# A pair of experts shares its 128 rows from both ends, in sixteen rounds instead of seventeen

## The chip, the cores and the metric

The kernel runs on one core of a Trainium2 chip. The metric is the device time of one execution in microseconds (us). The core has a matrix engine (TensorE, in the rows PE, with its weight loads as PEld), a vector engine (VectorE, DVE), a scalar engine (ScalarE, ACT), a general engine (GpSimd, POOL) and SyncE (SP), which here only issues DMAs. They run on their own and wait for one another by semaphores.

## What is computed

Two transformer layers on 512 tokens of 1024 features, all in float32. The change lies in the mixture of experts of the first layer; all else keeps its work. Cut to that:

```python
def hierarchical_moe(xn, w_rg, b_rg, w_re, b_re, w_gate, w_up, w_down):
    # 512 tokens; 4 groups of 8 experts; a token takes its best group and there the best 2 experts
    experts = (g_sel[:, None] * EXPERTS_PER_GROUP + top_i).astype(jnp.int32)      # 2 of 32 for each token
    ...
    def expert_block(args):
        xblk, e = args                                                            # rows of x, an expert
        hid = jax.nn.silu(xblk @ w_gate[e]) * (xblk @ w_up[e])                    # 1024 -> 512, twice
        return hid @ w_down[e]                                                    # 512 -> 1024
    ...
    y = jax.ops.segment_sum(yb * row_w[:, None].astype(yb.dtype), row_tok, num_segments=t + 1)[:t]
```

So 1024 pairs of token and expert fall on 32 experts, 32 on average. Worked out from the reference with these inputs, the fullest expert (number 5) has 74 tokens and all others have 64 or fewer; of the pairs (e, e + 16) the fullest has 93 tokens.

## The kernel before

**Weights.** All weights come from one array in units of 128 x 2048 floats (1 MB), in the order of use. An expert has six units (`PER_EXPERT`): two of the gate product, two of the up product, two of the down product.

**A round.** `expert_round` takes two neighbouring experts (`PAIR_UNITS` = 12 units, 12 MB, in `moe_w0` to `moe_w11`). Expert 2e has rows 0 to 63 of a block of 128 rows and expert 2e + 1 rows 64 to 127 (`CAP` = 64). PE turns the block of gathered rows (`turn_rows`, 8 transposes, line 741). In `up_units` each of 32 products (line 756) takes 64 columns of the turned rows `xe` as the held operand and streams 512 columns of a weight unit past it; the products of the two experts alternate and write to the two halves of the partitions of a bank. The gate sum stands in bank 2, the up sum in bank 3. ACT makes `gate` (silu, line 1357) as soon as the gate half is done, DVE multiplies it with bank 3 into `hid` (line 2036), PE turns `hid` (`turn_hidden`, 4 transposes, line 763), ACT and DVE each copy half of it into `hid_t` (lines 1362 and 2041), and `down_units` makes 16 products (line 779) into banks 5 and 6. ACT and DVE copy these to `y_rows`, and POOL scatters the rows to `pair_rows` (line 2477), each to the place of its pair of token and choice. A float32 product stands in the trace as two records of MATMUL, so a round has 64 and 32 of them.

**Where things are started.** SP reloads `moe_w` slot s for the next round when `unit_used` says that its unit of this round was used (line 494). POOL gathers the rows of round e + 2 (line 2467) when those of round e are turned. While the first sums of a round are made, the next round's rows are in `xe`: `turn_rows` of the next round stands between `up_units` and `turn_hidden`.

**The seventeenth round.** 16 rounds take all experts with up to 64 tokens each. What is over is cut into parts of up to 64 rows; a last round (`EXTRA`), which always runs, takes the first two parts, with its weights read again at addresses that SP loads from `over_int` (line 504). Without parts it would run on rows of no token. For more parts there is a branch, `overflowing`, with a loop of 14 turns over `over_weights`.

**Before the first round.** The router's numbers are made on DVE in a chain of small operations, each waiting for the one before (`chain`). The last of them is `dest`, the row of each pair in `slot_table`. POOL then writes the table with 8 indirect DMAs (line 2456), reads it back into `slots` with two DMAs (lines 2460 and 2461), issues the load of `over_slots` (line 2463), and gathers the first rows.

**After the last round** POOL waits for the scatters, SP loads `y_pairs`, and PE adds them to the residual (line 853). Then the second layer begins, whose weights are split into a rounded part and its rest (`w_hi`, `w_lo`) and multiplied three times (lines 556 to 558).

Of the kernel before, what the change touches and what calls it, by code (L numbers as in the profile page):

```python
# [49 lines left out]
U_HG = U_EXTRA + 2 * PER_EXPERT  # L50
# [9 lines left out]
EXTRA = NPAIR  # L60
ROUNDS = NPAIR + 1
PAIR_UNITS = 2 * PER_EXPERT
N_OVER = 14
# [8 lines left out]
def columns(*sizes):  # L72
    at, out = 0, {}
    for name, n in sizes:
# [5 lines left out]
                      ("sel", H1 * P), ("eps", 1), ("iota32", NE), ("lane", NE))  # L80
# [34 lines left out]
def build(nc, x_in, weights_in, constants_in, phase1_in, phase2_in, phase3_in, out):  # L115
    with ExitStack() as ctx:
# [75 lines left out]
        gate = place("gate", [FE], at_b + 16 * KB2)  # L192
        hid = place("hid", [FE], at_b + 17 * KB2)
        hid_t = place("hid_t", [4, P], at_b + 18 * KB2)
# [10 lines left out]
        def overflowing(eng):  # L205

            eng.wait_ge(dest_ready, 1)
            return eng.value_load(over_int[0:1, 2 + N_OVER:3 + N_OVER]) > 0

# [18 lines left out]
        over_cmp, over_e = tiny("over_cmp", [2 + N_OVER, NE]), tiny("over_e", [2 + N_OVER])  # L228
        over_int = tiny("over_int", [N_OVER + 3], I32)
# [11 lines left out]
        slot_table = nc.dram_tensor("slot_table", [MAIN + (2 + N_OVER) * CAP, 2], I32, kind="Internal").ap()  # L241
# [5 lines left out]
        TABLE = (MAIN + (2 + N_OVER) * CAP) * 2  # L247
# [182 lines left out]
        STORED_FROM, LANDED_FROM = 16 * (NPAIR // 2 + 1), 16 * (NPAIR // 2)  # L430
# [37 lines left out]
        def _(sp):  # L468
# [29 lines left out]
            sp.wait_ge(dest_ready, 1)  # L498
            over_unit = [sp.value_load(over_int[0:1, b:b + 1]) * PER_EXPERT + U_MOE for b in range(2)]
            for j in range(PER_EXPERT):  # L500
                for b in range(2):
                    s = 2 * j + b
                    sp.wait_ge(unit_used, U_EXTRA - PAIR_UNITS + s + 1)
                    sp.dma_start(moe_w[s][:], weights_in[bass.ds(over_unit[b] + j, 1)].rearrange("u p n -> p (u n)")) \
                        .then_inc(raw_landed[s], 16)

            for j in range(RAW):
                sp.wait_ge(unit_used, U_EXTRA + j + 1)
                sp.dma_start(raw[:, j], weights_in[U_EXTRA + j]).then_inc(raw_landed[j], 16)
# [38 lines left out]
        def _(pe):  # L548
# [196 lines left out]
            def up_units(e):  # L745

                for j in range(4):
# [39 lines left out]
            def expert_round(e, next_rows):  # L787
# [8 lines left out]
                pe.wait_ge(hid_ready, e + 1)  # L796
                turn_hidden()
# [4 lines left out]
            with pe.Fori(0, NPAIR // 2) as i:  # L802
                for b in range(2):
                    expert_round(i * 2 + b, (1 - b, i * 16 + 16 * (b + 1)))
            expert_round(EXTRA, None)


            with pe.If(overflowing(pe)):
                with pe.Fori(0, N_OVER) as v:
# [14 lines left out]
                    for c in range(4):  # L824
                        mm = nc.tensor.transpose(bank[4][:, c * P:c * P + P], hid[:, c * P:c * P + P], ident)
# [3 lines left out]
                    for c in range(4):  # L829
                        for half in range(2):  # L830
                            w = (c % 2) * D + half * 512
                            mm = nc.tensor.matmul(bank[5 + half][:], hid_t[:, c], over_weights[:, c // 2, w:w + 512],
# [1925 lines left out]
```

## Time and profile before

| | |
|---|---|
| time, median of 3 runs | 2318.77 us (2316.73 to 2321.3) |
| the profiled execution | 2321.49 us, of which the span is 2319.8 us |
| PE busy | 2080.0 us (90%), 10252 records of MATMUL |
| DVE, ACT, POOL busy | 39%, 29%, 16% |
| weights of the experts | 204 transfers of 1 MB, queued 25.2 us each (median) |
| first product of the experts, end of the last | 357.5 us, 874.2 us |

The profile cuts the span into 40 slices of 58 us. The experts fill slices 7 to 15; there the DMA engines are busy throughout and move 421 to 422 GB/s, while PE shows 7 to 8 tenths. Of the chain of work that ended last, 17% is the transfer of `moe_w`; nearly all else of it is PE.

### The profile page before, as it was taken

The page shows a single profiled execution, that of the slowest core. Times are in us where ns is not written, and L with a number is a line of the kernel's source. Part 1 is how long each engine was busy: PE and PEld are TensorE (multiplying, and loading weights), DVE is VectorE, ACT ScalarE, POOL GpSimd, SP SyncE. Part 2 cuts the span into 40 slices and gives each one's busy share as a digit, 9 for nine tenths or more (in the row PEclk, how much of TensorE's full clock was granted, in tenths as well). Part 3 has the DMA queues.
Part 4 walks back from the last instruction along what each step waited for, and adds up shares of the span by engine and source line. Part 5 has one row for each costly group of instructions (what it writes and reads, how often), then busy time and mean ns, then how long its engine had stood idle before and what let it go on. Part 6 is the DMA issues. An engine that isn't in the chain of part 4 may idle for free.

```text
span 2319.8 us, 25950 instructions
## 1 busy us (share of the span) xinstructions
PE 2080.0 (90%) x10252; PEld 1544.2 (67%) x10252; DVE 904.7 (39%) x1162; ACT 664.5 (29%) x840; POOL 363.3 (16%) x354
## 2 busy tenths in 40 slices
PE   6996828877777778999989999999999999999999
PEld 5894713322223227888867888887789987888887
DVE  5535250000000005677765432334775434333332
ACT  3433120000000004666644221223222323221222
POOL 0000020000000001554531110111343101100100
PEclk9997968999999999999989999999999999999999
DMA  5220247999999993121112222223222322222220
GB/s 203 78 105 0 86 181 305 421 422 421 421 421 421 421 410 154 55 73 55 55 62 91 91 95 104 91 90 109 91 74 98 140 73 91 91 91 98 96 97 37
DMA packets 57640, 378.10 MB, mean 163 GB/s; under 512 B 8944, under 2 KB 9040, under 8 KB 13904
## 3 DMA queue, kind: packets, MB, share of 16 engines
q1 hardware_dynamic: 51120, 363.02, 40.0%
q0 software_dynamic: 6432, 13.83, 1.7%
q8 instruction: 64, 1.05, 0.2%
q14 instruction: 24, 0.20, 0.0%
HBM read 370.99 MB, written 15.26 MB: 167 GB/s over the span
## 4 chain that ended last, share of the span: by engine, by line
PE 65%; DMA 18%; DVE 7%; issue 5%; ACT 3%; POOL 1%; SPq 0%; DVEq 0%; POOLq 0%; ACTq 0%
PE bank L556 18%; PE bank L557 18%; PE bank L558 18%; DMA moe_w<-weights_in 17%; PE bank L779 3%; PE bank L756 2%; DVE o_tmp L2185 1%; PE bank L853 1%; DVE k_dec L2161 1%; PE bank L675 1%; PE bank L1176 1%; POOL k_rot L2574 1%; PE bank L954 1%; PE bank L966 1%; DVE ws L2170 0%
## 5 line engine op out<-in xcount | busy, mean ns | idle before, releaser
L556 PE MATMUL bank<-u_hi,w_hi 128*128 128x512 f32 x1152 | 463.3, 402 | 0.7 <-issue 0.7
L557 PE MATMUL bank<-u_lo,w_hi 128*128 128x512 f32 x1152 | 455.5, 395 | 0.0
L558 PE MATMUL bank<-u_hi,w_lo 128*128 128x512 f32 x1152 | 455.1, 395 | 0.0
L1702 DVE TENSOR_TENSOR w_lo<-raw,w_hi 128x2048 fp32r<-128x2048 f32 x96 | 233.1, 2428 | 299.9 <-ACT w_hi L1227 299.7
L756 PE MATMUL bank<-moe_w,xe 128*64 128x512 f32 x1088 | 262.2, 629 | 88.9 <-DMA moe_w<-weights_in 87.7
L756 PEld LDWEIGHTS bank<-moe_w,xe 128*64 128x64 f32 x1088 | 91.1, 144 | 259.1 <-issue 259.0
L1227 ACT ACTIVATE w_hi<-raw 128x2048 fp32r<-128x2048 f32 x96 | 183.7, 1913 | 273.2 <-PE bank L558 272.3
L556 PEld LDWEIGHTS bank<-u_hi,w_hi 128*128 128x128 f32 x1152 | 216.5, 188 | 54.2 <-issue 3.5
L557 PEld LDWEIGHTS bank<-u_lo,w_hi 128*128 128x128 f32 x1152 | 216.5, 188 | 52.6 <-issue 2.4
L558 PEld LDWEIGHTS bank<-u_hi,w_lo 128*128 128x128 f32 x1152 | 216.2, 188 | 53.0
L556 PE MATMUL bank<-w_hi,u_hi 128*128 128x256 f32 (+1 forms) x640 | 191.5, 299 | 7.3 <-issue 7.3
L557 PE MATMUL bank<-w_lo,u_hi 128*128 128x256 f32 (+1 forms) x640 | 188.8, 295 | 0.0
L558 PE MATMUL bank<-w_hi,u_lo 128*128 128x256 f32 (+1 forms) x640 | 188.6, 295 | 0.0
L2563 POOL TENSOR_TENSOR f_gate<-f_gate,rms 128x512 f32<-128x512 f32 x44 | 57.0, 1296 | 566.5 <-ACT f_gate L1574 566.5
L2036 DVE TENSOR_TENSOR hid<-gate,bank 128x512 f32<-128x512 f32 x17 | 11.7, 689 | 339.0 <-PE bank L756 339.0
L779 PE MATMUL bank<-moe_w,hid_t 128*64 128x512 f32 x544 | 123.6, 596 | 17.8 <-ACT hid_t L1362 6.4
L556 PEld LDWEIGHTS bank<-w_hi,u_hi 128*128 128x128 f32 x640 | 122.0, 191 | 11.5 <-issue 8.3
L557 PEld LDWEIGHTS bank<-w_lo,u_hi 128*128 128x128 f32 x640 | 122.0, 191 | 3.2
L558 PEld LDWEIGHTS bank<-w_hi,u_lo 128*128 128x128 f32 x640 | 121.9, 190 | 3.1
L2280 DVE TENSOR_TENSOR f_hid<-f_gate,bank 128x512 f32<-128x512 f32 x44 | 30.3, 689 | 212.6 <-PE bank L558 212.6
L556 PE MATMUL bank<-hid_hi,w_hi 128*128 128x512 f32 x272 | 107.5, 395 | 0.1
L557 PE MATMUL bank<-hid_lo,w_hi 128*128 128x512 f32 x272 | 107.4, 395 | 0.0
(415 smaller groups left out, 2756.3 us busy)
## 6 DMA issues: line engine op xcount, KB each, us to landing
moe_w<-weights_in SPq DMA_DIRECT2D x204, 1024.0 KB, 25.2
raw<-weights_in SPq DMA_DIRECT2D x128, 1024.0 KB, 4.8
y_pairs<-pair_rows SPq DMA_DIRECT2D x4, 1024.0 KB, 7.7
res<-x_in SPq DMA_DIRECT2D x1, 2048.0 KB, 7.8
token_rows<-xn POOLq DMA_DIRECT2D x1, 2048.0 KB, 7.0
v_rows<-vals SPq DMA_DIRECT2D x2, 1024.0 KB, 5.7
vals<-v_rows SPq DMA_DIRECT2D x2, 1024.0 KB, 6.8
out<-out_tile SPq DMA_DIRECT2D x4, 512.0 KB, 2.6
```

Source lines behind the costliest of these rows:

```text
L556: nc.tensor.matmul(out_ap, a_hi, b_hi, start=first, stop=False)
L557: nc.tensor.matmul(out_ap, a_hi, b_lo, start=False, stop=False)
L558: return nc.tensor.matmul(out_ap, a_lo, b_hi, start=False, stop=last)
L675: mm = nc.tensor.matmul(bank[4 + b // 2][:, at:at + VH], dec_at(j, b * P, b * P + P), vm[:, j, h * VH:h * VH + VH], start=b % 2 == 0 and j ...
L756: mm = nc.tensor.matmul(bank[2 + j // 2][rows, :], xe[:, c, rows], moe_w[2 * j + b][:, w], start=c == 0, stop=c == KC - 1)
L779: mm = nc.tensor.matmul(bank[5 + half][rows, :], hid_t[:, c, rows], moe_w[2 * j + b][:, w], start=c == 0, stop=c == 3)
L853: mm = nc.tensor.matmul(of_block(c, b), y_pairs[b][:, k, c * P:c * P + P], share_diag[:, k, b], start=False, stop=b == TB - 1 and k == 1)
L954: mm = nc.tensor.matmul(bank[4 + n % 2][:, t], left, right, start=True, stop=True)
L1227: nc.scalar.activation(w_hi[:, n % 2], raw[:, n % RAW], ACT.Copy).then_inc(hi_ready, 1)
L1702: nc.vector.tensor_tensor(w_lo[:, n % 2], raw[:, n % RAW], w_hi[:, n % 2].bitcast(F32), ALU.subtract) \
L2280: nc.vector.tensor_tensor(f_hid[s][:], f_gate[s][:], bank[2 * s + 1][:], ALU.mult).then_inc(f_prod, 1)
L2563: nc.gpsimd.tensor_tensor(f_gate[n][:], f_gate[n][:], rms[:], ALU.mult).then_inc(f_gated, 1)
```

## The change

Experts e and e + 16 share a round. Expert e fills the 128 rows from the front, expert e + 16 from the back (constants `seat` and `stride`), each up to the `room` that is left, at least 64 rows. Both experts' products are made for all 128 rows: two gate banks (2, 3) and two up banks (4, 7). `mine` (1 or 0 for a row and an expert, from the number of rows of expert e) is multiplied in when `hid` is made, so that a row of the one expert gives zero in the `hid` of the other, and the down products of both add up in the same banks 5 and 6. The round `EXTRA` and its 12 transfers go, the branch for what is over (now 16 turns) stays, and the units of the two experts of a round are laid next to each other by the host.

```diff
-U_HG = U_EXTRA + 2 * PER_EXPERT
+U_HG = U_EXTRA
-ROUNDS = NPAIR + 1
+ROUNDS = NPAIR
...
-            sp.wait_ge(dest_ready, 1)
-            over_unit = [sp.value_load(over_int[0:1, b:b + 1]) * PER_EXPERT + U_MOE for b in range(2)]
-            for j in range(PER_EXPERT):
-                for b in range(2):
-                    s = 2 * j + b
-                    sp.wait_ge(unit_used, U_EXTRA - PAIR_UNITS + s + 1)
-                    sp.dma_start(moe_w[s][:], weights_in[bass.ds(over_unit[b] + j, 1)].rearrange("u p n -> p (u n)")) \
-                        .then_inc(raw_landed[s], 16)
...
                         for b in range(2):
-                            rows = slice(CAP * b, CAP * b + CAP)
-                            mm = nc.tensor.matmul(bank[2 + j // 2][rows, :], xe[:, c, rows], moe_w[2 * j + b][:, w],
+                            mm = nc.tensor.matmul(bank[(2 + b, 4 + 3 * b)[j // 2]][:], xe[:, c], moe_w[2 * j + b][:, w],
                                                   start=c == 0, stop=c == KC - 1)
...
-            def turn_hidden():
-                for c in range(4):
-                    mm = nc.tensor.transpose(bank[4 if c < 2 else 7][:, c % 2 * P:c % 2 * P + P], hid[:, c * P:c * P + P],
-                                             ident)
-                mm.then_inc(hid_turned, 1)
+            def turn_hidden(e):
+
+                for b in range(2):
+                    pe.wait_ge(hid_ready, e * 2 + b + 1)
+                    for c in range(4):
+                        mm = nc.tensor.transpose(bank[2 + b][:, c * P:c * P + P], hid[b][:, c * P:c * P + P], ident)
+                    mm.then_inc(hid_turned, 1)
...
                             for b in range(2):
-                                rows = slice(CAP * b, CAP * b + CAP)
-                                mm = nc.tensor.matmul(bank[5 + half][rows, :], hid_t[:, c, rows], moe_w[2 * j + b][:, w],
-                                                      start=c == 0, stop=c == 3)
+                                mm = nc.tensor.matmul(bank[5 + half][:], hid_t[b][:, c], moe_w[2 * j + b][:, w],
+                                                      start=c == 0 and b == 0, stop=c == 3 and b == 1)
...
                 act.wait_ge(unit_used, u0 + 4)
-                nc.scalar.activation(gate[:], bank[2][:], ACT.Silu).then_inc(silu_ready, 1)
+                for n in range(2):
+                    nc.scalar.activation(gate[n][:], bank[2 + n][:], ACT.Silu).then_inc(silu_ready, 1)
...
-                act.wait_ge(hid_turned, e + 1)
-                nc.scalar.activation(hid_t[:, 0:2], bank[4][:, 0:2 * P].rearrange("p (c t) -> p c t", c=2), ACT.Copy) \
+                act.wait_ge(hid_turned, e * 2 + 1)
+                nc.scalar.activation(hid_t[0][:], bank[2][:].rearrange("p (c t) -> p c t", c=4), ACT.Copy) \
                     .then_inc(hid_t_left, 1)
...
-                dve.wait_ge(silu_ready, e + 1)
                 dve.wait_ge(unit_used, u0 + 8)
-                nc.vector.tensor_tensor(hid[:], gate[:], bank[3][:], ALU.mult).then_inc(hid_ready, 1)
+                for n in range(2):
+                    dve.wait_ge(silu_ready, 2 * e + n + 1)
+                    nc.vector.scalar_tensor_tensor(hid[n][:], gate[n][:], mine[:, n, e:e + 1], bank[4 + 3 * n][:],
+                                                   ALU.mult, ALU.mult).then_inc(hid_ready, 1)
...
-                dve.wait_ge(hid_turned, e + 1)
-                nc.vector.tensor_copy(hid_t[:, 2:4], bank[7][:, 0:2 * P].rearrange("p (c t) -> p c t", c=2)) \
+                dve.wait_ge(hid_turned, 2 * e + 2)
+                nc.vector.tensor_copy(hid_t[1][:], bank[3][:].rearrange("p (c t) -> p c t", c=4)) \
                     .then_inc(hid_t_right, 1)
...
             pool.dma_start(slots[:, 0:NPAIR], slot_table[0:MAIN].rearrange("(s e) c -> s e c", s=P)).then_inc(slots_landed, 16)
-            pool.dma_start(slots[:, EXTRA], slot_table[MAIN:MAIN + P]).then_inc(slots_landed, 16)
-            pool.wait_ge(slots_landed, 48)
-            pool.dma_start(over_slots[0:CAP], slot_table[MAIN + P:].rearrange("(v s) c -> s v c", s=CAP)).then_inc(slots_landed, 16)
+            pool.wait_ge(slots_landed, 32)
...
             gather(0)
             gather(1)
+            pool.dma_start(over_slots[0:CAP], slot_table[MAIN:].rearrange("(v s) c -> s v c", s=CAP)).then_inc(slots_landed, 16)
```

The rounds on DVE, a loop before, are written out one by one. On PE, at the end of `up_units` in the loop of rounds, this stood in a row (`con` is the identity, `moe_w_103` and so on are the slots of weights, a row of a float32 product is one product, and its first shape is the held columns by the streamed ones):

```order
1310 L756 MATMUL bank<-moe_w_103,xe 64x512
1311 L756 MATMUL bank<-moe_w_104,xe 64x512
1312 L794 ISA
1313 L741 MATMUL bank<-con,x_rows 128x128 [waits x_gathered1]
1314 L741 MATMUL bank<-con,x_rows 128x128 x7
1315 L763 MATMUL bank<-con,hid 128x128 [waits hid_ready]
1316 L763 MATMUL bank<-con,hid 128x128 x3
1317 L779 MATMUL bank<-moe_w_105,hid_t 64x512 [waits raw_landed8,raw_landed9,hid_t_right,hid_t_left]
1318 L779 MATMUL bank<-moe_w_106,hid_t 64x512
```

The same place on PE now:

```order
1310 L746 MATMUL bank<-moe_w_106,xe 128x512
1311 L746 MATMUL bank<-moe_w_107,xe 128x512
1312 L785 ISA
1313 L732 MATMUL bank<-con,x_rows 128x128 [waits x_gathered1]
1314 L732 MATMUL bank<-con,x_rows 128x128 x7
1315 L754 ISA
1316 L756 MATMUL bank<-con,hid_95 128x128 [waits hid_ready]
1317 L756 MATMUL bank<-con,hid_95 128x128 x3
1318 L754 REGISTER_ALU
1319 L756 MATMUL bank<-con,hid_96 128x128 [waits hid_ready]
1320 L756 MATMUL bank<-con,hid_96 128x128 x3
1321 L770 MATMUL bank<-moe_w_108,hid_t_97 128x512 [waits raw_landed8,raw_landed9,hid_t_right,hid_t_left]
```

The number of products of a round is the same, all are 128 wide instead of 64, and a second set of four transposes with a wait of its own stands ahead of the down products. On DVE a round was, in the round `EXTRA` at the end (it turns no rows for a next round):

```order
268 L2036 TENSOR_TENSOR hid<-gate,bank 128x512 [waits unit_used,silu_ready]
269 L2041 COPY hid_t<-bank 128x256 [waits hid_turned]
270 L2045 COPY y_rows<-bank 128x512 [waits unit_used,y_free0]
```

The first round on DVE now:

```order
259 L2045 SCALAR_TENSOR_TENSOR hid_95<-gate_93,mine,bank 128x512 [waits silu_ready,unit_used]
260 L2045 SCALAR_TENSOR_TENSOR hid_96<-gate_94,mine,bank 128x512 [waits silu_ready]
261 L2036 COPY xe<-bank 128x512 [waits xe_turned]
262 L2051 COPY hid_t_98<-bank 128x512 [waits hid_turned]
263 L2055 COPY y_rows<-bank 128x512 [waits unit_used,y_free0]
```

Two products of 512 columns stand where one stood, and the copy into `hid_t` has 512 columns instead of 256. On POOL, from the last indirect writes of the table to the first gathers, before:

```order
14 L2456 DMA slot_table<-pairs,dest 3072x2 x7
15 L2460 DMA slots<-slot_table 128x32 [waits table_written]
16 L2461 DMA slots<-slot_table 128x2
17 L2463 DMA over_slots<-slot_table 64x14x2 [waits slots_landed]
18 L2467 DMA x_rows<-token_rows,slots 128x1024 x2
```

and now:

```order
14 L2464 DMA slot_table<-pairs,dest 3072x2 x7
15 L2468 DMA slots<-slot_table 128x32 [waits table_written]
16 L2473 DMA x_rows<-token_rows,slots 128x1024 [waits slots_landed]
17 L2473 DMA x_rows<-token_rows,slots 128x1024
18 L2480 DMA over_slots<-slot_table 64x16x2
```

One read of the table is gone, and the other that isn't needed at once stands behind the gathers. On DVE the six operations that make the numbers for what is over stood ahead of `dest`; they now stand behind it, with the ones that make `mine`, and six other small ones (for `room`, and `row` in two steps) are new in the chain ahead of it.

## Rows read from the trace of the kernel before

**Rows 1.** The page: busy tenths, clock and DMA in 40 slices.

```profile
PE   6996828877777778999989999999999999999999
...
PEclk9997968999999999999989999999999999999999
DMA  5220247999999993121112222223222322222220
GB/s 203 78 105 0 86 181 305 421 422 421 421 421 421 421 410 154 55 73 55 55 62 91 91 95 104 91 90 109 91 74 98 140 73 91 91 91 98 96 97 37
```

**Rows 2.** Chain of work that ended last, in order of time: start, us, what.

```profile
357.53 16.45 PE bank L756 x64
...
420.88 5.20 PE bank L756 x16
...
494.20 3.67 PE bank L779 x16
498.65 27.14 DMA moe_w<-weights_in
525.92 3.67 PE bank L779 x16
...
840.17 3.67 PE bank L779 x16
844.49 25.94 DMA moe_w<-weights_in
870.57 3.67 PE bank L779 x16
```

**Rows 3.** Timeline: start, us, engine, line, operation, count, idle before; a round without DMA waits.

```profile
383.06 13.93 PE L756 MATMUL bank<-moe_w,xe 128*64 128x512 f32 x64
...
400.00 7.09 PE L779 MATMUL bank<-moe_w,hid_t 128*64 128x512 f32 x32 [0.72 <-ACT hid_t L1362]
...
406.89 7.07 PE L756 MATMUL bank<-moe_w,xe 128*64 128x512 f32 x32
```

**Rows 4.** Timeline of PE: a float32 product with 128 held and 512 streamed columns.

```profile
920.38 1.88 PE L996 MATMUL bank<-late_diag,con 128*128 128x512 f32 x4
```

**Rows 5.** The instructions of line 756, then of 779: duration in ns min/median/max.

```profile
L756 PE MATMUL bank<-moe_w,xe x1088: 592/592/1116, 357.5 to 863.7; 128*64 128x512 f32 x182
...
L779 PE MATMUL bank<-moe_w,hid_t x544: 592/592/644, 376.2 to 873.6; 128*64 128x512 f32 x182
```

**Rows 6.** Timeline of one handoff from the up to the down products.

```profile
426.01 1.09 PE L741 MATMUL bank<-con,x_rows 128*128 128x128 f32 x8
426.14 0.69 DVE L2036 TENSOR_TENSOR hid<-gate,bank 128x512 f32<-128x512 f32 x1 [18.32 <-PE bank L756]
...
426.94 0.60 PE L763 MATMUL bank<-con,hid 128*128 128x128 f32 x4
427.14 0.60 ACT L1350 ACTIVATE xe<-bank 128x512 f32<-128x512 f32 x1 [12.55 <-PE bank L741]
427.14 0.69 DVE L2028 COPY xe<-bank 128x512 f32<-128x512 f32 x1 [0.31 <-PE bank L741]
427.64 0.38 ACT L1362 ACTIVATE hid_t<-bank 128x256 f32<-128x256 f32 x1
427.75 0.41 DVE L2041 COPY hid_t<-bank 128x256 f32<-128x256 f32 x1
...
428.27 1.94 PE L779 MATMUL bank<-moe_w,hid_t 128*64 128x512 f32 x8 [0.72 <-ACT hid_t L1362]
```

**Rows 7.** Timeline ahead of the first round: DVE, then POOL.

```profile
331.07 0.69 DVE L1993 TENSOR_TENSOR over_cmp<-over_end,con 128x512 f32<-128x512 f32 x1
...
333.31 0.17 DVE L2002 CAST dest<-dest_f 128x8 int32<-128x8 f32 x1
...
346.87 0.56 POOL L2461 DMA_DIRECT2D slots<-slot_table  x1
349.20 0.82 POOL L2463 DMA_DIRECT2D over_slots<-slot_table  x1 [1.77 <-DMA slots<-slot_table]
350.33 1.07 POOL L2467 DMA_INDIRECT x_rows<-token_rows,slots  x1 [0.30 <-issue]
```

**Rows 8.** Scatters of line 2477, issue to landing; the last of them is in the chain at 875.89.

```profile
DMA to landing us min/median/max: 5.1/8.3/9.1
```

More of the change, by code:

```diff
@@ L59 @@
 NPAIR = NE // 2
-EXTRA = NPAIR
-ROUNDS = NPAIR + 1
+ROUNDS = NPAIR
 PAIR_UNITS = 2 * PER_EXPERT
-N_OVER = 14
+N_OVER = 16
 MAGIC = 12582912.0
@@ L191, in build @@
         xe = place("xe", [KC, P], at_b + 12 * KB2)
-        gate = place("gate", [FE], at_b + 16 * KB2)
-        hid = place("hid", [FE], at_b + 17 * KB2)
-        hid_t = place("hid_t", [4, P], at_b + 18 * KB2)
+        gate = [place(f"gate{b}", [FE], at_b + (16 - 2 * b) * KB2) for b in range(2)]
+        hid = [place(f"hid{b}", [FE], at_b + (17 - 2 * b) * KB2) for b in range(2)]
+        hid_t = [place(f"hid_t{b}", [4, P], at_b + (18 + b) * KB2) for b in range(2)]
         y_rows = place("y_rows", [2, D], at_b + 20 * KB2)
@@ L824, in _ @@
                     for c in range(4):
-                        mm = nc.tensor.transpose(bank[4][:, c * P:c * P + P], hid[:, c * P:c * P + P], ident)
+                        mm = nc.tensor.transpose(bank[4][:, c * P:c * P + P], hid[0][:, c * P:c * P + P], ident)
                     mm.then_inc(over_products, 1)
@@ L1366, in expert_round @@
                 nc.scalar.activation(y_rows[:, b, 0:512], bank[5][:], ACT.Copy).then_inc(y_left, 1)
-            with act.Fori(0, NPAIR // 2) as i:
+            with act.Fori(0, NPAIR // 2 - 1) as i:
                 for b in range(2):
                     expert_round(i * 2 + b, i * (2 * PAIR_UNITS) + (U_MOE + PAIR_UNITS * b), b, i * 16 + 16, False)
-            expert_round(EXTRA, U_EXTRA, 0, 16 * (NPAIR // 2 + 1), True)
+            for b in range(2):
+                expert_round(NPAIR - 2 + b, U_EXTRA - PAIR_UNITS * (2 - b), b, 16 * (NPAIR // 2), b == 1)
             split(U_HG)
@@ L1381, in _ @@
                     act.wait_ge(over_products, v * 4 + 2)
-                    nc.scalar.activation(gate[:], bank[2][:], ACT.Silu).then_inc(over_copies, 1)
+                    nc.scalar.activation(gate[0][:], bank[2][:], ACT.Silu).then_inc(over_copies, 1)
                     act.wait_ge(over_products, v * 4 + 3)
-                    nc.scalar.activation(hid_t[:], bank[4][:].rearrange("p (c t) -> p c t", c=4), ACT.Copy) \
+                    nc.scalar.activation(hid_t[0][:], bank[4][:].rearrange("p (c t) -> p c t", c=4), ACT.Copy) \
                         .then_inc(over_copies, 1)
@@ L1974, in _ @@
             before, count = before_all[:], so_far[:, TB - 1]
-            chain(nc.vector.tensor_scalar(n_over[:], count, 1.0, -0.5 - CAP / 2, ALU.max, ALU.add))
+            for n in range(2):
+                last = nc.vector.tensor_scalar(room[:, n * NPAIR:(n + 1) * NPAIR], count[:, (1 - n) * NPAIR:(2 - n) * NPAIR],
+                                               -1.0, float(P), ALU.mult, ALU.add)
+            chain(last)
+            chain(nc.vector.tensor_scalar(room[:], room[:], float(CAP), None, ALU.max))
+            chain(nc.vector.tensor_tensor(n_over[:], count, room[:], ALU.subtract))
+            chain(nc.vector.tensor_scalar(n_over[:], n_over[:], 1.0 - CAP, CAP / 2 - 0.5, ALU.max, ALU.add))
             chain(nc.vector.tensor_scalar(n_over[:], n_over[:], 1.0 / CAP, MAGIC, ALU.mult, ALU.add))
@@ L1980, in _, with per_token @@
             chain(nc.vector.tensor_tensor(over_start[:], over_end[:], n_over[:], ALU.subtract))
-            chain(nc.vector.tensor_scalar(over_start[:], over_start[:], float(CAP), float(MAIN - CAP), ALU.mult, ALU.add))
-            chain(nc.vector.tensor_scalar(over[:], before, float(CAP), None, ALU.is_ge))
-            chain(nc.vector.tensor_tensor(lift[:], before, over_start[:].unsqueeze(1).to_broadcast([P, TB, NE]), ALU.add))
-            lane = cols(con, C_COLS, "lane").unsqueeze(1).to_broadcast([P, TB, NE])
-            chain(nc.vector.scalar_tensor_tensor(row[:], before, float(NPAIR), lane, ALU.mult, ALU.add))
+            chain(nc.vector.tensor_scalar(over_start[:], over_start[:], float(CAP), float(MAIN), ALU.mult, ALU.add))
+            chain(nc.vector.tensor_tensor(over_start[:], over_start[:], room[:], ALU.subtract))
+            def per_token(tile):
+                return tile.unsqueeze(1).to_broadcast([P, TB, NE])
+            nc.vector.tensor_tensor(over[:], before, per_token(room[:]), ALU.is_ge)
+            nc.vector.tensor_tensor(lift[:], before, per_token(over_start[:]), ALU.add)
+            chain(nc.vector.tensor_tensor(row[:], before, per_token(cols(con, C_COLS, "stride")), ALU.mult))
+            chain(nc.vector.tensor_tensor(row[:], row[:], per_token(cols(con, C_COLS, "seat")), ALU.add))
             chain(nc.vector.tensor_tensor(lift[:], lift[:], row[:], ALU.subtract))
@@ L2045, in expert_round @@
                 nc.vector.tensor_copy(y_rows[:, b, 512:1024], bank[6][:]).then_inc(y_right, 1)
-            with dve.Fori(0, NPAIR // 2) as i:
-                for b in range(2):
-                    expert_round(i * 2 + b, i * (2 * PAIR_UNITS) + (U_MOE + PAIR_UNITS * b), b, i * 16 + 16, False)
-            expert_round(EXTRA, U_EXTRA, 0, 16 * (NPAIR // 2 + 1), True)
+            for e in range(NPAIR):
+                expert_round(e, U_MOE + PAIR_UNITS * e, e % 2, 16 * (e // 2 + 1), e == NPAIR - 1)
             split(U_HG)
@@ L2057, in _ @@
                     dve.wait_ge(over_copies, v * 4 + 2)
-                    nc.vector.tensor_tensor(hid[:], gate[:], bank[3][:], ALU.mult).then_inc(over_hid, 1)
+                    nc.vector.tensor_tensor(hid[0][:], gate[0][:], bank[3][:], ALU.mult).then_inc(over_hid, 1)
             for b in range(TB):
```

62 lines of the change are left out of this document (34 added, 28 removed).

## The prediction

> **What bounds the kernel now.** I read the slices of the page first: in slices 7 to 15, the experts, the DMA engines are busy throughout at 421 to 422 GB/s while PE shows 7 to 8 tenths [rows 1]. So I went to the chain of work that ended last, in order of time. From the third round on it is made of one pattern: 26 to 27 us of moe_w transfers, then the 16 records of the last down unit [rows 2]. From 494.20 to 840.17 there are eleven such rounds, 345.97 / 11 = 31.45 us each: the rate at which 12 MB of weights arrive. The PE work of a round is smaller. Where no transfer is awaited, the 64 records of the up products start at 383.06 and last 13.93 us, and the 32 of the down products take 406.89 - 400.00 = 6.89 us from their first start to the first start of the next round [rows 3]. With the handoff between them (below, 2.26 us) that makes some 23 us of PE against 31.45 us of DMA, 8 us of slack in a round. What matters is what the change does to these 23 us.
>
> **Part 1: the products become 128 wide.** This is the large term. In the kernel before, 32 records of 64 held columns take 6.89 us, 0.215 us a record [rows 3]. One record of itself lasts 592 ns [rows 5], and the two experts' records alternate and write different halves of the partitions: they run beside each other. The same product with 128 held columns stands once in the trace: four records of line 996 in 1.88 us, which is three distances and one duration of 0.592 us, so (1.88 - 0.59) / 3 = 0.43 us a record [rows 4]. That is twice the 0.215, which is what two streams side by side against one would give. The change leaves the count of products alone and makes all of them 128 wide, so nothing can run beside them: 96 records x 0.43 = 41.3 us a round, where it was 20.6. That rows 4 has four records only is a weakness of this term; the bounds below take it in.
>
> A rule of the Trainium skill speaks against this. "TensorE: Matmul & The Clock Gate", section "Back-to-back issue gap", gives a sustained rate of about 131 ns for a 512-column matmul in a real stream, less than its formula for one alone; and "FP8 and Floating Point Precision" counts four passes for a true float32 product, two for each of our records. By these, an estimate, a record would cost 262 ns and a round 96 x 0.262 = 25.2 us of products, which would still lie under the transfers. The trace disagrees as far as it goes (0.43 us in rows 4).
>
> **Part 2: the handoff from up to down.** Before, it is 428.27 - 426.01 = 2.26 us from the first transpose of the next rows to the first down product [rows 6]. Now, from that transpose as zero and with the durations of these rows: hid of the first expert on DVE from 0.13 to 0.82, that of the second right behind until about 1.43, xe's copy until about 2.05; PE turns the second hid from 1.54 (DVE's end plus the 0.11 that the rows show between 426.83 and 426.94); its copy can start 0.70 later, as ACT's did (426.94 to 427.64), at 2.24, and takes 0.69 us for 512 columns, as xe's does; PE starts 0.11 after that, at 3.04. ACT's two copies of 0.60 end by then. The second silu lies under the up products, which now take 27 us. So 3.0 us, +0.8. Bounds: 2.3, if DVE's parts overlap more than I think, and 4.5, if a semaphore costs more.
>
> **A round** is then 41.3 + 3.0 = 44.3 us of PE, against 31.45 us of transfers. Transfers are no longer awaited: each slot is refilled from the moment it was used, and its next use comes a round, 44 us, later; the gathers have over 27 us. The 8 us of slack and the 31.45 us of the removed round are gone against 12.9 us more in each of sixteen rounds.
>
> **Part 3: the sum of the stage.** 16 x 44.3 = 708.8 us. The first round starts on a PE that has idled: its 64 records took 16.45 us against 13.93 at the full clock [rows 2, 3], +2.5 us, and I keep that, since the clock comes back by time. 711.3 us, where the kernel before has 870.57 + 3.67 - 357.53 = 516.7 us [rows 2]. That is **+194.6 us**.
>
> **Part 4: ahead of the first round.** dest no longer waits for the six operations between 331.07 and 333.31 (2.24 us); six others of 0.22 us on average (some of 128 elements, 0.3) are in its chain, +1.3. The read of slots that lands last was issued 0.56 us after the first, and over_slots held up the gather from 349.20 to 350.33, 1.13 us [rows 7]. Together -0.9 - 0.6 - 1.1 = **-2.6 us**; nothing else was late there, for PE had all weights of the round. The work that is now behind dest has 20 us until DVE is wanted. Bounds: -1 and -3.5.
>
> **Part 5: behind the last round.** The last scatter takes 5.1 us, the smallest of all, on the seventeenth round, which holds 10 rows of tokens; it will hold 93. The median of 8.3 comes from a time when the DMA engines were full [rows 8]. I take 5.8, **+0.7 us**, bounds 0 and 3.2. The wider table of constants and the written-out loop on DVE I take as nothing: DVE waits most of a round, and if fetching its code were late by a microsecond, that would stand in the handoff's bound.
>
> **Sum:** +194.6 - 2.6 + 0.7 = +192.7 us. The profiled execution took 2321.49 us (span 2319.8), so by its own time 2514.2; the median of the runs shown is 2.7 us lower, 2318.77, and so I forecast **2511.5 us**.
>
> **The rivals.**
>
> *Wide products cost less, and DMA stays the bound.* If a record of 128 held columns cost under (31.45 - 3.0) / 96 = 0.296 us, the round would be hidden under its transfers, and the change would do nothing but take one round away: 2318.8 - 31.45 - 1 (part of the start) + 0.7 (the last scatter) = 2287 us. For it speaks that what a record of 592 ns shares with its neighbour isn't shown by any row, and the rule above. Against it stands rows 4. This is the case on the other side; it decides at 0.296 us a record. 4%.
>
> *The clock falls in every handoff.* The handoff becomes 3 us of transposes and waiting. In the kernel before the clock does fall now and then after a wait: 16 records took 5.20 us instead of 3.67 [rows 2], 1.5 us lost, and the longest record of line 756 is 1116 ns. With such a fall in each of the sixteen rounds it is 16 x 1.5 = +24 us, 2536 us. Against it: in 17 rounds no down product, which come right behind the handoff, was over 644 ns [rows 5], and the up products behind these ran at full speed at 406.89 [rows 3]. The skill's page on TensorE, section "Part 4: PE-mode transpose", says that transposes don't count as busy for the clock gate, which would speak for this rival; the rows of the 17 handoffs do not bear it out. 8%.
>
> *The branch for what is over is taken.* It would run 16 turns with 6 MB each, one behind the other: at 421 GB/s 15 us of transfers, and 48 records x 0.43 = 21 us of products, some 36 us or more a turn, +570 us. The loads of the experts speak against it: the fullest pair has 93 tokens of 128. 1%.
>
> *The forecast:* PE bounds the stage at about 44 us a round. 87%.
>
> **The numbers.** Around the likeliest: the price of a record from 0.427 to 0.435 us gives -5 to +8; the handoff's bounds -11 to +24; start and tail -1.6 to +4. They will not all fall on one side. With the rival of the clock the range is **2499 to 2542 us**. What it leaves out is the case of cheap products (4%), the branch (1%), and the edges of the rest. Chances: faster by over 0.2% 4%, within 0.2% (about what a measurement of this kernel can tell from no change) 1%, slower by more 95%.
>
> **What would show it.** The product rows of the two lines should read 128*128 with a distance of 0.43 us, so busy times of about 440 us for up (1024 records) and 220 us for down (512). The idle time of PE that transfers end should all but vanish from the stage; the bandwidth there should fall from 421 to about 12.6 MB / 44.3 us = 284 GB/s plus the rows, and the transfers should land sooner than 25 us after their issue. PE's share in these slices should be 9 tenths at the full clock. First to last product: about 711 us. It would be wrong if the wide records stood closer than 0.43 us, if the handoff were not near 3 us, or if the clock in the stage were clearly under full.

## The result: 2514.7 us, 8.4% slower

| | median | runs | lowest to highest |
|---|---|---|---|
| before | 2319.39 us | 4 | 2316.73 to 2321.3 |
| after | 2514.66 us | 4 | 2513.03 to 2517.4 |

The ratio is 1.0844, with a 95% interval of 1.0825 to 1.0863. The forecast was 2511.5 us, with a range of 2499 to 2542.

### The profile page after: what moved, and what is told of

Same layout as the page of the kernel before. It is cut to its first block, busy times and chain, and to the rows that moved or that the text cites. A ratio compares the mean times of both kernels' runs of the same rounds, so it can differ in the third digit from the quotient of the medians.

```text
span 2515.6 us, 25808 instructions
## 1 busy us (share of the span) xinstructions
PE 2372.2 (94%) x10208; PEld 1715.7 (68%) x10208; DVE 917.8 (36%) x1184; ACT 673.2 (27%) x851; POOL 364.4 (14%) x351
## 4 chain that ended last, share of the span: by engine, by line
PE 47%; DVE 4%; issue 4%; ACT 2%; POOL 0%; DMA 0%; DVEq 0%; POOLq 0%
PE bank L547 14%; PE bank L549 14%; PE bank L548 14%; DVE o_tmp L2193 1%; DVE k_dec L2169 1%; PE bank L844 1%; PE bank L1167 1%; PE bank L945 1%; PE bank L957 0%; POOL k_rot L2581 0%; DVE ws L2178 0%; PE bank L1115 0%; ACT L1481 0%; PE bank L1112 0%; PE bank L903 0%
## 5 line engine op out<-in xcount | busy, mean ns | idle before, releaser
L746 PE MATMUL bank<-moe_w,xe 128*128 128x512 f32 x1024 | 444.1, 595 | 1.2 <-DVE xe L2036 1.2
L746 PEld LDWEIGHTS bank<-moe_w,xe 128*128 128x128 f32 x1024 | 195.9, 191 | 246.4 <-issue 246.4
L770 PE MATMUL bank<-moe_w,hid_t 128*128 128x512 f32 x512 | 223.6, 595 | 13.3 <-ACT hid_t L1354 13.3
L770 PEld LDWEIGHTS bank<-moe_w,hid_t 128*128 128x128 f32 x512 | 96.3, 190 | 131.2 <-issue 114.5
L2045 DVE SCALAR_TENSOR_TENSOR hid<-gate,mine,bank 128x512 f32<-128x512 f32 x32 | 22.5, 745 | 430.6 <-PE bank L746 430.6
L2484 POOL DMA_INDIRECT pair_rows<-y_rows,slots x16 | 16.1, 1006 | 685.0 <-DVE y_rows L2055 685.0
```

What stands on the lines that cost most here:

```text
L746: mm = nc.tensor.matmul(bank[(2 + b, 4 + 3 * b)[j // 2]][:], xe[:, c], moe_w[2 * j + b][:, w], start=c == 0, stop=c == KC - 1)
L770: mm = nc.tensor.matmul(bank[5 + half][:], hid_t[b][:, c], moe_w[2 * j + b][:, w], start=c == 0 and b == 0, stop=c == 3 and b == 1)
```

## The profile after

The page of the changed kernel, with the rows that answer to [rows 1]: busy tenths of PE, granted clock and DMA in 40 slices, each now 63 us.

```profile
PE   6995749999999999999999999999999999999999
...
PEclk9997879999999999999999999999999999999999
DMA  4220337877777777431112122222312322222221
GB/s 187 95 74 36 144 141 282 310 299 283 305 286 301 295 290 302 169 140 51 67 68 74 51 101 85 99 99 85 118 68 100 116 86 86 99 91 93 101 84 51
```

In slices 7 to 16, which the experts fill, PE shows 9 tenths where it had 7 or 8, the granted clock is at 9 tenths or more, and the DMA engines are at 7 or 8 tenths with 282 to 310 GB/s where they had up to 422. The two have changed places as the bound. In the chain that ended last, moe_w's transfers, 17% before, no longer appear: the page has

```profile
PE 47%; DVE 4%; issue 4%; ACT 2%; POOL 0%; DMA 0%; DVEq 0%; POOLq 0%
...
L746 PE MATMUL bank<-moe_w,xe 128*128 128x512 f32 x1024 | 444.1, 595 | 1.2 <-DVE xe L2036 1.2
...
L770 PE MATMUL bank<-moe_w,hid_t 128*128 128x512 f32 x512 | 223.6, 595 | 13.3 <-ACT hid_t L1354 13.3
...
moe_w<-weights_in SPq DMA_DIRECT2D x192, 1024.0 KB, 6.4
```

(line, engine, operation, shapes and count | busy us, mean ns | idle before it and what ended it; the last line is KB and us from issue to landing). The shares of the chain do not add up to the span, which it only follows back through the second layer; the groups are the better reading here. The products of a record are 128 wide, their busy times are 444.1 and 223.6 us, and of the idle time ahead of them no part was ended by a transfer of weights. A transfer lands 6.4 us after its issue instead of 25.2.

The timeline of the second round answers to [rows 3] and [rows 6]: start, us, engine, line, operation.

```profile
383.91 1.04 PE L732 MATMUL bank<-con,x_rows 128*128 128x128 f32 x8
384.11 1.41 DVE L2045 SCALAR_TENSOR_TENSOR hid<-gate,mine,bank 128x512 f32<-128x512 f32 x2 [30.00 <-PE bank L746]
384.91 1.31 PE L756 MATMUL bank<-con,hid 128*128 128x128 f32 x8
384.98 0.60 ACT L1341 ACTIVATE xe<-bank 128x512 f32<-128x512 f32 x1 [13.52 <-PE bank L732]
385.43 0.68 DVE L2036 COPY xe<-bank 128x512 f32<-128x512 f32 x1
385.61 0.60 ACT L1354 ACTIVATE hid_t<-bank 128x512 f32<-128x512 f32 x1
386.26 0.69 DVE L2051 COPY hid_t<-bank 128x512 f32<-128x512 f32 x1
387.06 13.97 PE L770 MATMUL bank<-moe_w,hid_t 128*128 128x512 f32 x32 [0.83 <-ACT hid_t L1354]
400.87 27.63 PE L746 MATMUL bank<-moe_w,xe 128*128 128x512 f32 x64
...
428.33 1.04 PE L732 MATMUL bank<-con,x_rows 128*128 128x128 f32 x8
```

The 64 up records last 27.63 us, (27.63 - 0.59) / 63 = 0.429 us from one to the next; the handoff is 387.06 - 383.91 = 3.15 us; a round is 428.33 - 383.91 = 44.4 us.

**Where the 195.8 us of span came from**, by the two profiled executions (spans of 2319.8 and 2515.6 us):

| stretch | before | after | difference |
|---|---|---|---|
| start to the first product of the experts | 357.5 | 354.5 | -3.1 |
| first to last product of the experts | 516.7 | 712.9 | +196.2 |
| last product to the first of y_pairs | 12.8 | 11.1 | -1.7 |
| from there to the end (second layer) | 1432.8 | 1437.1 | +4.3 |

The last row stands at work that the change does not touch. It got runs of its own.

## The experiments

Ten kernels ran. The kernel before was timed beside each group of them (medians of 2317.8 to 2320.6 us).

**1. The width alone taken back.** All of the change but the width of the products (this kernel is called narrow below):

```diff
-mm = nc.tensor.matmul(bank[(2 + b, 4 + 3 * b)[j // 2]][:], xe[:, c], moe_w[2 * j + b][:, w],
+rows = slice(CAP * b, CAP * b + CAP)
+mm = nc.tensor.matmul(bank[(2 + b, 4 + 3 * b)[j // 2]][rows, :], xe[:, c, rows], moe_w[2 * j + b][:, w],
...
-mm = nc.tensor.matmul(bank[5 + half][:], hid_t[b][:, c], moe_w[2 * j + b][:, w], start=c == 0 and b == 0, ...)
+mm = nc.tensor.matmul(bank[5 + half][rows, :], hid_t[b][:, c, rows], moe_w[2 * j + b][:, w], start=c == 0, ...)
```

> The changed kernel with its sixteen rounds, its two gate, up and hidden banks and all else, but each product 64 wide again: expert e for rows 0 to 63, expert e + 16 for rows 64 to 127 (the rows of expert 5 beyond 64 are left out of its products). This takes the width alone back. Theory (the width makes the +196 us of the stage, all else is small and a gain): the stage is bound by its transfers again, 16 x 31.45 us with the faster first rounds, about 485 us where it was 712.9, so 2514.7 - 712.9 + 485 = 2287 us; the handoff of 3.1 us, the second hidden bank and the written-out loop are covered. Rival (part of the loss is in the handoff and the doubled work of DVE and ACT): above 2300 us.

Measured: 2294.23 us, ratio 0.9884 (0.9868 to 0.9901). The width is the loss; all else of the change together is a gain of 1.2%. That is under the rival's bound of 2300, but 7 us over the 2287 I gave. The trace has the stage at 354.1 to 841.0, 486.9 us, close to the 485. The rest is behind it. The last scatter came while transfers of the next stage's weights still filled the DMA engines (the last was issued at 820.8 us, with 25.2 us to landing), and POOL waited 5.66 us after its issue where it waited 3.44 in the changed kernel; and the second layer was long again (1439.1 us; see experiment 6). The timeline of narrow, then of the changed kernel:

```profile
842.70 0.99 POOL L2486 DMA_INDIRECT pair_rows<-y_rows,slots  x1 [29.42 <-DVE y_rows L2057]
...
849.34 0.10 POOL L2512 MEMSET y_mark<- 128x8 int32 x1 [5.66 <-issue]
```

```profile
1069.06 0.99 POOL L2484 DMA_INDIRECT pair_rows<-y_rows,slots  x1 [43.42 <-DVE y_rows L2055]
...
1073.49 0.10 POOL L2510 MEMSET y_mark<- 128x8 int32 x1 [3.44 <-issue]
```

**2. Narrow records without a neighbour.** Both experts' products to rows 0 to 63 (`rows = slice(0, CAP)`).

> The changed kernel with 64 wide products, but both experts' products go to rows 0 to 63 (rows 64 to 127 are left out). The records have the same shape as in the kernel before, 128*64 by 128x512, and their number is the same, but none has a neighbour in the other half of the array. Theory (0.215 us a record is two streams side by side at 0.43 each, the price hangs on streamed columns and passes, not on the held width): 0.43 us a record, about 2515 us, as the changed kernel. Rival (a record with 64 held columns is cheaper in itself): 0.215 us a record, 2287 us.

Measured: 2513.56 us (two runs, 2512.80 and 2514.32), the changed kernel's time. Its timeline has records of the same shape as in the kernel before, at the price of the wide ones:

```profile
429.45 13.92 PE L772 MATMUL bank<-moe_w,hid_t 128*64 128x512 f32 x32 [0.83 <-ACT hid_t L1356]
...
443.20 27.63 PE L747 MATMUL bank<-moe_w,xe 128*64 128x512 f32 x64
```

So a record with 64 held columns and no neighbour is no cheaper than one with 128. The 0.215 us a record of the kernel before were two streams of 0.43 us in the two halves of the array, as the theory had it. The rival is out by 226 us.

**3. The halves one after the other.**

```diff
-for k in range(4):
-    for b in range(2):
+for b in range(2):
+    for k in range(4):
```

(the same in the down products, on top of experiment 1).

> As narrow, with the halves of both experts, but a unit's products of expert e all come first and then those of expert e + 16 (8 records of one half, then 8 of the other), instead of by turns. Theory (records only run beside a neighbour in the other half that comes right behind, in order): only the records at a change of half overlap, about 96 x 7/8 x 0.43 = 36 us of products a round, 39 with the handoff, 2514.7 - 712.9 + 16 x 39.3 + 2 = 2433 us. Rival one (matmuls are taken out of order over 8 records): 2287 us. Rival two (no overlap is left at all): 2515 us.

Measured: 2295.96 us (2292.87 and 2299.05). My theory, that only neighbours in the program run beside each other, is wrong by 137 us. Rival one gave the right time, but not quite for its reason. The weight loads of the down products (start, busy, count in a row; each belongs to a record, and the first row holds the loads of the first two):

```profile
489.60 0.19 PEld L772 LDWEIGHTS bank<-moe_w,hid_t 128*64 128x64 f32 x2 [1.04 <-ACT hid_t L1356]
490.08 0.14 PEld L772 LDWEIGHTS bank<-moe_w,hid_t 128*64 128x64 f32 x1 [0.29 <-issue]
490.51 0.14 PEld L772 LDWEIGHTS bank<-moe_w,hid_t 128*64 128x64 f32 x1 [0.29 <-issue]
490.94 0.14 PEld L772 LDWEIGHTS bank<-moe_w,hid_t 128*64 128x64 f32 x1 [0.29 <-issue]
491.37 0.19 PEld L772 LDWEIGHTS bank<-moe_w,hid_t 128*64 128x64 f32 x3 [0.29 <-issue]
491.80 0.19 PEld L772 LDWEIGHTS bank<-moe_w,hid_t 128*64 128x64 f32 x2 [0.23 <-issue]
492.23 0.19 PEld L772 LDWEIGHTS bank<-moe_w,hid_t 128*64 128x64 f32 x2 [0.23 <-issue]
```

The first four distances of 0.43 us bring one record each; then they come in twos, though eight records of one half stand ahead of the first of the other. Records of one half do not run beside each other (experiment 2). So the first record of the second half starts with the fifth of the first half, ahead of three that stand before it in the program, and from there both halves are busy. So little is lost. A round that waits for no transfer takes 424.94 - 398.83 = 26.1 us by its first transposes, against 23.8 by turns (experiment 5):

```profile
398.83 1.09 PE L732 MATMUL bank<-con,x_rows 128*128 128x128 f32 x8
...
424.94 1.09 PE L732 MATMUL bank<-con,x_rows 128*128 128x128 f32 x8
```

Where 16 up records wait for a transfer they take 5.39 us against 3.65, since each such group starts with one half alone. The idle time of PE that transfers end ahead of the up products shrinks from 75.2 us in narrow to 12.4 us here. The transfers are still the bound, and so the time does not move. That PE's queue holds a few records for each half is my reading of this row of counts; the runs show the overlap and its four records, not how it is made.

**4. The width alone added to the kernel before.** `matmul(bank[2 + j // 2][:], xe[:, c], ...)` in its seventeen rounds.

> The kernel before with its seventeen rounds and only the products made 128 wide (both experts' products are made for all rows and add up in the one bank, so the sums are not those of the reference). The width alone, without the rest of the change. Theory: 17 x (41.3 + 2.3) + 2 = 743 us of stage where it was 516.7, so 2319 + 226 = 2545 us. Rival (wide products cost so much only with the changed banks): less than 2500 us.

Measured: 2538.61 us (2537.87 and 2539.36), ratio 1.0946 (1.0926 to 1.0966). The chain of work that ended last, in order of time, has the rounds at 43.47 us where 43.6 was expected:

```profile
403.50 27.47 PE bank L755 x64
446.97 27.47 PE bank L755 x64
490.44 27.47 PE bank L755 x64
```

The stage is 741.8 us (743 expected). Most of the 6 us that are missing are behind the stage: 10.6 us to the first y_pairs product instead of 12.8, and 1428.0 us from there instead of 1432.8. With experiment 1 this gives all four cases:

| | seventeen rounds | sixteen rounds |
|---|---|---|
| 64 wide | 2319 | 2294 |
| 128 wide | 2539 | 2515 |

The width costs 220 us with either number of rounds. The rest of the change brings 24 to 25 us at either width. At 64 wide that is above all one round of transfers (31 us) less; at 128 wide it is one round of PE (43 us) less, against sixteen longer handoffs.

**5. A quarter of the transfers.** From the second round on `moe_w[s][:, 0:512]` alone is loaded.

> The changed kernel, but from the second round on each transfer of weights brings only 512 of the 2048 columns of its unit (the others keep the first round's weights). It asks whether transfers still bound any part of the stage. Theory (PE alone bounds it): nothing moves, 2513 to 2517 us. Rival (PE's reads of weights and the DMA writes get in each other's way, or some unit is still awaited): some us faster, 2505 or less.

Measured: 2515.32 us (2514.92 and 2515.72). A quarter of the bytes leaves the time where it was: transfers bound nothing in the changed kernel, and their writes at some 300 GB/s cost PE nothing that can be seen.

> As narrow (64 wide, expert 5's rows beyond 64 left out), with a quarter of the weights' transfer from the second round on. It shows PE's own time of a narrow round. Theory: 96 x 0.215 + 3.1 = 23.7 us a round, stage 16 x 23.7 + 2 = 381 us, 2514.7 - 712.9 + 381 = 2183 us, and so 7.7 us of slack a round in narrow. Rival (ACT and DVE, or the gathers and scatters, come up as the next bound): above 2200 us.

Measured: 2187.71 us (2186.87 and 2188.56), 5 us over the theory's figure and under the rival's 2200. The rounds are 464.36 - 440.55 = 23.8 us by their first transposes:

```profile
440.55 1.09 PE L733 MATMUL bank<-con,x_rows 128*128 128x128 f32 x8
...
464.36 1.09 PE L733 MATMUL bank<-con,x_rows 128*128 128x128 f32 x8
```

PE's own round is 23.8 us when narrow and 44.4 when wide, and the transfers' round of 31.45 us lies between them. That is the whole case: of the 20.6 us that the change adds to a round of PE, the first 7.6 were free, and the other 13.0 were paid sixteen times.

**6. Four microseconds at 128 bytes.** The second layer took 4.3 us longer in the changed kernel, and 1 to 6 us longer in all kernels of the experiments above that were made from it (the 4 to 6 in the next expectation leaves out the two shortest). Its products of line 548, `hid_lo` by `w_hi`, have a mean of 397 ns where the kernel before has 395. The one thing that had changed for them was the place of arrays: the table of constants grew from 1345 to 1378 columns, and all that is placed behind it moved by 128 bytes in each partition (places are rounded to 32 bytes). So 33 unused columns went into the kernel before:

```diff
-                      ("sel", H1 * P), ("eps", 1), ("iota32", NE), ("lane", NE))
+                      ("sel", H1 * P), ("eps", 1), ("iota32", NE), ("lane", NE), ("pad", 33))
```

> The kernel before with 33 unused columns behind its table of constants, as many as the change adds. Nothing reads them; they move the parameters and the arrays behind them by 128 bytes in each partition. In all kernels made from the changed one the three products of lines 547 to 549 last 397 ns where they last 394 to 395 in the kernel before, and the time from the first y_pairs product to the end is 4 to 6 us longer. Theory (the moved addresses do it): 394 becomes 397 here too, and the time is 4 us longer, 2323 to 2324 us. Rival (chips differ, or something else of the change): no change beyond 1 us for the longer load of constants.

Measured: 2322.66 us in 11 runs (2320.30 to 2323.54) against 2318.77 in 15 (2316.23 to 2321.26), ratio 1.0015 (1.0006 to 1.0024). And the other way round, the changed kernel with its three new tables put where nothing moves:

> The changed kernel with seat, stride and index moved from the table of constants into the second table of parameters, which is shorter than the room it has, and the first table padded to its former size, so that every array stands at the address that it has in the kernel before. Theory (addresses): 394 ns again and 4 us less, about 2511 us. Rival: 2515 us.

Measured: 2507.26 us (2506.51 to 2508.90), 7.4 us less than the changed kernel, more than expected. The two were not timed side by side; against the kernel before beside each, the ratios are 1.0811 (1.0795 to 1.0828) and 1.0844 (1.0825 to 1.0863), so the size of this difference is known less well than that of the 3.9 us above. The groups of this one product, of the kernel before, then with the pad, of the changed kernel, and of it with the tables moved:

```profile
L557 PE MATMUL bank<-hid_lo,w_hi 128*128 128x512 f32 x272 | 107.4, 395 | 0.0
```

```profile
L557 PE MATMUL bank<-hid_lo,w_hi 128*128 128x512 f32 x272 | 107.8, 396 | 0.0
```

```profile
L548 PE MATMUL bank<-hid_lo,w_hi 128*128 128x512 f32 x272 | 107.9, 397 | 0.0
```

```profile
L549 PE MATMUL bank<-hid_lo,w_hi 128*128 128x512 f32 x272 | 107.5, 395 | 0.0
```

The effect is shown; its cause is not. The starts in the traces give its size. In the second layer some 4470 records stream 512 columns of an array of activations (`u`, `hid` and the like) past a held piece of `w_hi` or `w_lo`. They stand 233.3 ns apart in all four kernels with the tables in their first place, and 234.2 ns in all eight where they are moved: 0.9 ns each, 4.0 us in all, which is what the pad costs. The activations lie behind the table and moved; `w_hi` and `w_lo` lie ahead of it and did not. The 231 records of 512 columns that stream a weight past held activations do not get slower (233.3 and 233.1 ns). That points at the place of the streamed array, but no run moved one array alone. Of the 7.4 us of the kernel with the tables put back, these records explain 4.0; the rest is not explained. Single profiled executions scatter by about 3 us around this: the second layer is 1428.0 to 1434.6 us long in the four with the tables in their first place, and 1434.1 to 1439.1 in the eight where they are moved, so the reading rests on the timed medians.

**7. A version that beats both.** Only a round in which an expert has over 64 rows needs wide products, here one of sixteen. DVE makes a flag for each pair from its counts, and PE takes one of two bodies; the other engines do the same in both, since `mine` makes the rows of the wrong expert zero whatever stands in the bank there. All that the reference asks for is computed.

```diff
+            chain(nc.vector.tensor_tensor(wide_f[:], count[:, 0:NPAIR], count[:, NPAIR:], ALU.max))
+            chain(nc.vector.tensor_scalar(wide_f[:], wide_f[:], CAP + 0.5, None, ALU.is_gt))
+            chain(nc.vector.tensor_copy(wide[:], wide_f[:]))
...
+                with pe.If(pe.value_load(wide[0:1, at]) > 0):
+                    body(False)
+                with pe.Else():
+                    body(True)
```

> A version meant to beat both: the changed kernel, with all it computes, but PE looks at the start of a round at a flag that DVE made from the counts (1 where one of the two experts has over 64 rows) and takes either a body with 128 wide products or one with 64 wide ones; all other engines do the same in both. With these inputs one round of sixteen is wide (experts 5 and 21). Theory: the transfers bound the stage, and even the wide round keeps the queue of transfers full (some 10 MB are outstanding when it begins), PE makes up for its 44 us in the rounds behind it: 2287 us, as narrow. Rival one: the wide round adds its 13 us over a round of transfers, 2300 us. Rival two: loading the flag and the branch hold PE for several us in each round, more than the 8 us of slack: above 2319 us.

Measured: 2294.73 us (2291.97 to 2295.66), ratio 0.9895 (0.9879 to 0.9912), where narrow had 2294.23 and 0.9884 (0.9868 to 0.9901). No difference from narrow can be seen, as the theory had it, and like narrow it is over the theory's figure, by 8 us. With the tables put as in experiment 6:

> The version with a wide or a narrow body chosen for each round, and the tables placed as in after_placed. Theory (addresses): 4 us less than chosen's 2294.7, so about 2290.5 us, ratio 0.988. Rival: unchanged.

Measured: 2287.99 us (2285.79 to 2290.32), ratio 0.9862 (0.9847 to 0.9877), 1.4% faster than before and 9% faster than the changed kernel. Its timeline shows the wide round and what comes behind it:

```profile
525.03 13.97 PE L774 MATMUL bank<-moe_w,hid_t 128*128 128x512 f32 x32 [0.83 <-ACT hid_t L1366]
538.93 13.96 PE L749 MATMUL bank<-moe_w,xe 128*64 128x512 f32 x64
...
555.91 7.09 PE L774 MATMUL bank<-moe_w,hid_t 128*64 128x512 f32 x32 [0.83 <-ACT hid_t L1366]
562.80 10.50 PE L749 MATMUL bank<-moe_w,xe 128*64 128x512 f32 x48
...
574.79 3.65 PE L749 MATMUL bank<-moe_w,xe 128*64 128x512 f32 x16 [1.49 <-DMA moe_w<-weights_in]
```

The wide round leaves PE behind its transfers; the next one runs from end to end without a wait, in 562.80 - 538.93 = 23.9 us from its first up record to the first of the round behind it, and in that one the first wait for a transfer comes again. The 13 us are made up for.

## Why the prediction was right

**The bound of the kernel before** was read rightly: 31.45 us of transfers over 23 us of PE in a round. Experiment 5 measures the second number, 23.8 us with the longer handoff. One reading was too broad: the DMA engines are at 421 to 422 GB/s in slices 8 to 14 only; [rows 1] has 305 in slice 7 and 410 in slice 15. The chain, on which the bound rests, is not touched by that. Of that chain PE has 65% and `moe_w` 17%; DVE has 7% and "issue" 5%, so PE is most of the rest, not nearly all.

**Part 1**, wide products: 0.43 us a record was expected from four records of line 996, 0.429 came. The explanation by streams side by side holds too (experiment 2). The Trainium skill's sustained rate of 131 ns for 512 columns in "TensorE: Matmul & The Clock Gate" (section "Back-to-back issue gap") is not borne out by any product here: two passes of it would be, an estimate, 262 ns a record, where these stand 429 ns apart, and the split products of the second layer, also of 512 columns, stand 233 ns apart. The four passes for true float32 in the Trainium skill's "FP8 and Floating Point Precision" (section "TensorE Precision Notes"), two in each record, would make 429 / 2 = 214 ns a pass here, somewhat under the 233 ns and far from 131.

**Part 2**, the handoff: 3.0 us expected, 3.15 measured, in the order that was laid out. Both products on DVE took 1.41 us, 0.1 more than two with a start of 0.61 between them.

**Part 3**, the stage: +194.6 expected, +196.2 measured. A round was 44.4 us instead of 44.3; the first, on a PE that had waited, cost 29.60 - 27.63 = 2.0 us more instead of 2.5. The granted clock of its first 5.5 us is 0.66.

**Part 4**, the start: -2.6 expected, -3.1 measured, and not quite for the reasons given. `dest` came 2.0 us sooner (331.29 instead of 333.31), but 0.9 of that was there before the changed operations began (`so_far` is first written at 324.37 instead of 325.24); the operations themselves brought 1.1, where 0.9 was expected. From the first read of the table to the first gather it is 2.8 us instead of 4.0, 1.3 less where 1.7 was expected. The gather and the steps behind it took 0.2 more. The 0.9 is in no term, and no run says where it comes from.

**Part 5**, the last scatter: +0.7 expected, -1.7 measured. The sign was wrong. I took the 5.1 us of the kernel before as those of idle DMA engines and added for more rows. But four transfers of the next stage had been issued there until 856.46, with 25.0 us to landing, so they reached into the scatter at 875.89; in the changed kernel such transfers land in some 6 us. There the scatter of 93 rows takes 3.3 us, the smallest of its sixteen. Experiment 3 bears this out: its transfers are still slow, but by about 848 us they had landed (the last was issued at 823.4, with 24.2 us to landing), and for the scatter issued at 847.44 POOL again waited 3.44 us and not narrow's 5.66. The scatters of the changed kernel:

```profile
DMA to landing us min/median/max: 3.3/6.6/7.6
```

**What stood in no term:** the 4 us of the moved tables. I named the wider table and priced it at nothing. The sum of +192.7 against the span's +195.8 is 3 us short, and the pieces of that are +1.6, -0.5, -2.4 and +4.3. That the sum is so close is in part luck: the wrong sign of part 5 and the table that had no price stand against each other, and so, in part, do the errors inside part 4. The stage, nearly all of the sum, is no luck: its round was right in each of its two terms.

**The rivals.** The clock did not fall in the handoffs. Its mean over the stage is 1.00, which is the upper level, 2.4 GHz (stretch in us; its length; busy us and count of PE, PEld, DVE, ACT, POOL; clock, DMA share, GB/s):

```profile
354.50:1067.00 712.50, 698.33 (x1784) 319.70 (x1785) 52.96 (x78) 53.28 (x85) 29.43 (x29) 1.00 0.73 282
```

No down record was over 669 ns. The Trainium skill's "TensorE: Matmul & The Clock Gate" (section "Part 4: PE-mode transpose") says that transposes do not count as busy in the same way; that made no difference in these sixteen handoffs of 3.15 us. The branch for what is over was not taken. The case of cheap wide products is out by the 0.429 us a record, and by experiment 4 with other banks.

## What to carry to other kernels

Two products of 64 held columns in the two halves of the array cost together what one of 64 or of 128 held columns costs alone (0.43 us a record here). Making both full width doubles PE's time, whatever rows of theirs are in use. Ahead of such a change, compare PE's own round with the transfers' round; the change is free up to the gap between them (here 7.6 us) and costs in full beyond it (here 13.0 us in each of sixteen rounds). And when a rare case asks for the expensive form, the engine can choose for each round: here the branch and one expensive round in sixteen were hidden behind the transfers.

## What the runs showed of the hardware that was not expected

- Halves of the array run beside each other even when 8 records of one stand in the program ahead of 8 of the other; the second joins after four distances of 0.43 us, ahead of records that stand before it in the program (experiment 3).
- Arrays moved by 128 bytes in each partition made the kernel 3.9 us slower (2318.77 to 2322.66, ratio 1.0006 to 1.0024). Some 4470 records that stream a moved array stand 234.2 ns apart instead of 233.3, which is all of it. Two other kernels were 6.7 and 7.4 us faster with the arrays put back, of which these records explain 4.0. Why the place matters is open.
- One wide round of PE (494.34 to 538.93, 44.6 us, in the last kernel of experiment 7) amid rounds of 31.45 us of transfers cost nothing that the times show, since the next ran in 23.9 us.
